# A two-block transformer kernel: x and ctx turned ahead of the first modulation, two projection chunks in the first stage

## The reference

```python
mod = (silu_c @ w_ada[l] + b_ada[l])[:, None, :]      # for x
mod_c = silu_cc @ w_ada[l] + b_ada[l]                 # for ctx
sh_a, sc_a, gt_a, sh_f, sc_f, gt_f = jnp.split(mod, 6, axis=-1)
csh_a, csc_a, ... = jnp.split(mod_c, 6, axis=-1)
h = rms_norm(x, g_attn[l]) * (1.0 + sc_a) + sh_a      # 256 tokens x 2048
hc = rms_norm(xc, g_attn[l]) * (1.0 + csc_a) + csh_a  # 256 tokens x 2048
pl, pc = h @ w_in, hc @ w_in                          # 2048 x 4928, split into q, k, v of four mixers
```

## Time and profile before

| | |
|---|---|
| three runs | 2822.24, 2824.46, 2827.69 us |
| span of the profiled execution | 2822.8 us |
| time of the profiled execution | not listed apart from its span |
| PE busy | 2748.1 us, 97% |
| VectorE busy | 1766.0 us, 63% |
| ScalarE busy | 1162.0 us, 41% |
| GpSimd busy | 388.5 us, 14% |
| moved by DMA | 579 MB, mean 205 GB/s |

### The profile page before, as it was taken

One profiled execution on the slowest core, in us unless ns is written; L12 is line 12 of the kernel. 1 busy time (PEld: TensorE's weight loads), 2 busy tenths in 40 slices (PEclk: granted clock), 3 DMA queues, 4 the chain that ended last, 5 costly groups with the idle time before them and its releaser, 6 DMA issues.

```text
span 2822.8 us, 33207 instructions
## 1 busy us (share of the span) xinstructions
PE 2748.1 (97%) x12531; PEld 2220.7 (79%) x12531; DVE 1766.0 (63%) x1952; ACT 1162.0 (41%) x1508; POOL 388.5 (14%) x297
## 2 busy tenths in 40 slices
PE   4999999999999999999999999999999999999998
PEld 1588887587887888888888888888888888888887
DVE  2379974766889655555574556544565656556566
ACT  3132224544444344444454544444444444444444
POOL 2214504101777200000040000000000000000000
PEclk9999999999999999999999999999999999999999
DMA  9988983246877555555555543655565656556663
GB/s 353 339 262 311 322 276 119 76 176 195 274 264 250 193 186 194 188 194 190 193 198 191 168 159 120 224 194 194 179 197 185 193 188 190 182 189 193 193 193 120
DMA packets 286236, 579.02 MB, mean 205 GB/s; under 512 B 14098, under 2 KB 18626, under 8 KB 283966
## 3 DMA queue, kind: packets, MB, share of 16 engines
q1 hardware_dynamic: 277240, 542.55, 58.1%
q0 software_dynamic: 7040, 34.29, 3.6%
q10 hardware_dynamic: 1862, 0.92, 0.1%
HBM read 572.59 MB, written 5.14 MB: 205 GB/s over the span
## 4 chain that ended last, share of the span: by engine, by line
PE 87%; DVE 5%; issue 4%; DMA 2%; POOLq 1%; POOL 1%; ACT 0%; DVEq 0%; SPq 0%; ACTq 0%
PE bank L367 27%; PE bank L369 26%; PE bank L368 26%; DVE w_lo L363 3%; DMA w_raw<-in_w_ada 1%; PE bank L628 1%; DMA b_rows<-in_b_ada 1%; PE bank L938 1%; PE bank L1943 1%; PE bank L460 1%; PE bank L790 0%; PE bank L654 0%; PE bank L827 0%; PE bank L1952 0%; PE bank L588 0%
## 5 line engine op out<-in xcount | busy, mean ns | idle before, releaser
L363 DVE TENSOR_TENSOR w_lo<-w_raw,w_hi 128x1024 fp32r<-128x1024 f32 (+2 forms) x856 | 1136.1, 1353 | 529.8 <-ACT w_hi L355 528.5
L355 ACT ACTIVATE w_hi<-w_raw 128x1024 fp32r<-128x1024 f32 (+2 forms) x856 | 889.0, 1054 | 1156.4 <-PE bank L369 1000.0
L367 PE MATMUL bank<-w_hi,xa_hi 128*128 128x512 f32 (+1 forms) x2304 | 905.9, 393 | 7.8 <-DVE w_lo L363 4.8
L369 PE MATMUL bank<-w_hi,xa_lo 128*128 128x512 f32 (+1 forms) x2304 | 895.6, 389 | 0.0
L368 PE MATMUL bank<-w_lo,xa_hi 128*128 128x512 f32 (+1 forms) x2304 | 895.1, 388 | 0.0
L367 PEld LDWEIGHTS bank<-w_hi,xa_hi 128*128 128x128 f32 x2304 | 433.2, 188 | 108.2 <-DVE w_lo L363 9.2
L369 PEld LDWEIGHTS bank<-w_hi,xa_lo 128*128 128x128 f32 x2304 | 433.1, 188 | 90.1
L368 PEld LDWEIGHTS bank<-w_lo,xa_hi 128*128 128x128 f32 x2304 | 433.3, 188 | 87.2 <-issue 0.7
L367 PE MATMUL bank<-w_hi,ffn_act_hi 128*128 128x512 f32 x800 | 311.5, 389 | 0.2 <-DVE w_lo L363 0.2
L368 PE MATMUL bank<-w_lo,ffn_act_hi 128*128 128x512 f32 x800 | 311.2, 389 | 0.0
L369 PE MATMUL bank<-w_hi,ffn_act_lo 128*128 128x512 f32 x800 | 311.2, 389 | 0.0
(11 more groups left out here) (306 smaller groups left out, 2037.7 us busy)
## 6 DMA issues: line engine op xcount, KB each, us to landing
w_raw<-in_w_in SPq DMA_DIRECT2D x116, 1024.0 KB, 5.1
w_raw<-in_w_ada SPq DMA_DIRECT2D x80, 1024.0 KB, 7.3
w_raw<-in_w_up SPq DMA_DIRECT2D x64, 1024.0 KB, 5.6
w_raw<-in_w_down SPq DMA_DIRECT2D x64, 1024.0 KB, 5.0
w_raw<-in_ffn_wg SPq DMA_DIRECT2D x44, 1024.0 KB, 5.2
w_raw<-in_ffn_wu SPq DMA_DIRECT2D x44, 1024.0 KB, 5.2
w_raw<-in_ffn_wd SPq DMA_DIRECT2D x44, 1024.0 KB, 5.1
w_raw<-in_w_out SPq DMA_DIRECT2D x32, 1024.0 KB, 5.1
```

The source lines that it names most:

```text
L355: act.activation(whi[:, slot, ks, 0:w], raw[:, q, ks, 0:w], ACT.Copy)\
L363: dve.tensor_tensor(wlo[:, slot, ks, 0:w], raw[:, q, ks, 0:w], whi[:, slot, ks, 0:w].bitcast(F32), ALU.subtract).then_inc(sem("lo_made"), 1)
L367: pe.matmul(out, xh, wh, start=first, stop=False)
L369: return pe.matmul(out, xl, wh, start=False, stop=last)
```

## The change

The two lists of the first stage change: each of four groups has two ada chunks, then the quarter of chunk 1 and that of chunk 0. Chunk 1 (512 columns, two token tiles, banks 6 and 7) leaves the mixed stage. x and ctx are scaled by VectorE, turned by PE without modulation into banks 0 to 3, 6 and 7, and copied to SBUF by ScalarE, all during the first two ada chunks. The scale and shift sums of a chunk are copied by ScalarE as rows; PE turns them into columns by four small products; VectorE adds b_ada and makes the scale (now one number per partition) and modulates turned x and ctx in place, 128 x 256 at a time. ScalarE then copies the high part and VectorE subtracts, from SBUF. The spread, GpSimd's products, the broadcast of g_attn and the b_ada rows are gone; g_attn and b_ada come in as 48 rows of 128 ahead of the identity and x on SP's queue, and are turned with c. The ada products alternate between banks 4 and 5.

```diff
-U_OUT = U_MIX + 4 * (len(WIN) - 1) + 4 * N_LATE_D + 4
+U_OUT = U_MIX + 4 * (len(WIN) - 2) + 4 * N_LATE_D + 4
...
-    for c in range(N_ADA_1):
-        if c >= 2 and c % 2 == 0:
-            loads.append(("win", 0, c // 2 - 1))
-        loads += [("ada", c, q) for q in range(4)]
-    return loads + [("win", 0, 3)]
+    for g in range(4):
+        loads += [("ada", c, q) for c in (2 * g, 2 * g + 1) for q in range(4)]
+        loads += [("win", 1, g), ("win", 0, g)]
+    return loads
...
-BY_VECTOR = {1: (1, 1, 1, 1), 2: (1, 1, 2, 1), 3: (1, 1, 1, 1), 4: (2, 2, 2, 2), 5: (2, 2, 2, 2), 6: (2, 3, 2, 3), 7: (3, 3, 3, 0)}
+PIECES = {g: [(1, 0), (1, 1), (0, 0), (1, 2), (1, 3), (0, 1), (0, 2), (0, 3)] for g in range(3)} | \
+    {3: [(1, 0), (1, 1), (0, 0), (0, 1), (0, 2), (0, 3), (1, 2), (1, 3)]}
+EARLY_BANK = {0: 0, 1: 6}
+EARLY_TOKS = {0: (0, 1, 2, 3), 1: (0, 1)}
+def early_count(w, g, j):
+    return 8 * g + PIECES[g].index((w, j)) + 1
+BY_VECTOR = {2: (2, 2, 2, 2), 3: (1, 1, 1, 1), 4: (2, 2, 2, 2), 5: (2, 2, 2, 3), 6: (2, 3, 2, 3), 7: (3, 3, 3, 0)}
```

On SP, when a slot is free again (`front_read`):

```diff
-                sp.wait_ge(sem("ada_used" if kind == "ada" else "early_lo"), 4 * c + q + 1 if kind == "ada" else 2 * q + 2)
+                if kind == "ada":
+                    sp.wait_ge(sem("ada_used"), 4 * c + q + 1)
+                else:
+                    sp.wait_ge(sem("early_lo"), 4 * q + (2 if c == 1 else 4))
...
+        def early_lo(dve, w, g, h):
+            q = FRONT.index(("win", w, g)) % 4
+            dve.wait_ge(sem("early_hi"), 4 * g + (1 if w == 1 else 3) + h)
+            dve.tensor_tensor(wlo[:, w, 2 * h:2 * h + 2, :], raw[:, q, 2 * h:2 * h + 2, :],
+                              whi[:, w, 2 * h:2 * h + 2, :].bitcast(F32), ALU.subtract).then_inc(sem("early_lo"), 1)
+        def early_piece(pe, w, g, j):
+            pe.wait_ge(sem("h_lo"), 2 * g + (1 if w == 1 else 2))
+            pe.wait_ge(sem("early_lo"), 4 * g + (1 if w == 1 else 3) + j // 2)
...
+        def modulate(dve, g, v):
+            for k in range(4 * g, 4 * g + 4):
+                m = dve.tensor_scalar(xt[v][:, k, :], xt[v][:, k, :], s_col[:, k, v:v + 1], b_col[:, k, v:v + 1],
+                                      ALU.mult, ALU.add)
+            m.then_inc(sem("h_made"), 1)
```

On ScalarE:

```diff
+            rows(0)
+            turn_x_act(act, 0)
+            turn_x_act(act, 1)
+            rows(1)
+            turn_x_act(act, 2)
+            turn_x_act(act, 3)
             for g in range(4):
-                early_hi(act, g)
-                turn_h_act(act, g)
+                if g:
+                    rows(2 * g)
+                    rows(2 * g + 1)
+                early_hi(act, 1, g)
+                h_hi(act, g, 0)
+                h_hi(act, g, 1)
+                early_hi(act, 0, g)
...
                 if i < 2:
-                    act.wait_ge(sem("early_used"), 4 * i + 12)
+                    act.wait_ge(sem("early_used"), early_count(i, 3, 3))
...
+                if i == 1:
+                    win_copy(1)
```

On VectorE:

```diff
+            for g in range(4):
+                take(2 * g)
+                take(2 * g + 1)
+                dve.wait_ge(sem("xt_copied"), 4 * g + 4)
+                modulate(dve, g, 0)
+                modulate(dve, g, 1)
+                early_lo(dve, 1, g, 0)
+                h_lo(dve, g, 0)
+                early_lo(dve, 1, g, 1)
+                h_lo(dve, g, 1)
+                early_lo(dve, 0, g, 0)
+                early_lo(dve, 0, g, 1)
```

On PE:

```diff
+            for q in range(4):
+                ada_unit(0, q)
+            columns(0)
+            for q in range(4):
+                ada_unit(1, q)
+                if q:
+                    turn_x_pe(pe, q - 1)
+            columns(1)
+            turn_x_pe(pe, 3)
+            pe.wait_ge(sem("xt_copied"), 16)
+            for g in range(3):
+                rest = list(PIECES[g])
+                for u in range(8):
+                    c, q = 2 * g + 2 + u // 4, u % 4
+                    ada_unit(c, q)
+                    if u < 5 or u == 7:
+                        w, j = rest.pop(0)
+                        early_piece(pe, w, g, j)
+                    if q == 3:
+                        columns(c)
+                for w, j in rest:
+                    early_piece(pe, w, g, j)
+            for w, j in PIECES[3]:
+                early_piece(pe, w, 3, j)
```

More of the change, by code:

```diff
@@ L95, in mixed_units @@
     units = []
-    for c in range(1, len(WIN)):
+    for c in range(2, len(WIN)):
         for q in range(4):
@@ L416, in early_piece @@
             m.then_inc(sem("early_used"), 1)
-        def turn_bank(g, i):
-            return 4 if g == 3 and i % 2 else 7
-        def turn_h_pe(pe, g, i):
-            pe.wait_ge(sem("h_ready"), 4 * g + i + 1)
-            wait(pe, "h_lo", 4 * g + i - (g == 3 and i >= 2))
-            for j in range(4):
-                m = pe.transpose(ps[turn_bank(g, i)][:, j * P:j * P + P],
-                                 xin[:, i, (4 * g + j) * P:(4 * g + j + 1) * P], ident[:, :])
-            m.then_inc(sem("h_turned"), 1)
@@ L448, in build, with h_lo @@
+        def h_lo(dve, g, v):
+            dve.wait_ge(sem("h_hi"), 2 * g + v + 1)
+            dve.tensor_tensor((XA, XB)[v][1][:, 4 * g:4 * g + 4, :], xt[v][:, 4 * g:4 * g + 4, :],
+                              (XA, XB)[v][0][:, 4 * g:4 * g + 4, :].bitcast(F32), ALU.subtract).then_inc(sem("h_lo"), 1)
         TURN = {"h2": range(8), "mrg": [0, 1, 2, 3, 2, 3, 4, 5], "h3": [2, 3, 6, 7, 6, 7, 4, 5], "h4": [4, 5, 6, 7] * 2}
@@ L1643, in _ @@
-            early_lo(dve, 3)
-            take(N_ADA_1 - 1)
-            for i in range(4):
-                turn_h_dve(dve, 3, i)
+                    .then_inc(sem("late_row"), 1)
+            dve.wait_ge(sem("x_rstd"), 1)
+            for g in range(4):
+                for i in range(4):
+                    x = xin[:, i, g * NCH:(g + 1) * NCH]
+                    dve.tensor_scalar(x, x, stat(RSTD + i), None, ALU.mult).then_inc(sem("x_scaled"), 1)
+            for g in range(4):
+                take(2 * g)
[9 more added lines that the diff above has]
+                early_lo(dve, 0, g, 1)
@@ L1944, in ada_unit, with columns @@
                                   start=q == 0, stop=q == 3)
                 m.then_inc(sem("ada_used"), 1)
-            def spread_row(c):
+            def columns(c):
                 pe.wait_ge(sem("ada_rows"), c + 1)
-                wait(pe, "mod_row", c)
-                for v in range(2):
-                    m = pe.matmul(ps[5 + v][:, :], pick[:, v:v + 1].to_broadcast([P, P]),
-                                  rows_1[:, c % 2, :], start=True, stop=True)
-                m.then_inc(sem("ada_combined"), 1)
@@ L1974, in _ @@
-            early_piece(pe, 2, 2)
-            spread_row(N_ADA_1 - 1)
-            early_piece(pe, 2, 3)
-            for i in range(4):
-                turn_h_pe(pe, 3, i)
-            for j in range(4):
-                early_piece(pe, 3, j)
+                for k in range(4):
+                    m = pe.matmul(ps[4 + c % 2][:, 2 * k:2 * k + 2], rows_1[:, c % 2, k * P:k * P + P], pick[:, :],
+                                  start=True, stop=True)
+                m.then_inc(sem("ada_columns"), 1)
@@ L2033, in _ @@
                     if cx is not None:
[L2034 removed]
+                        wait(pe, "late_row", sum(f < i for f in FOLD_AT))
                 toks = (0, 1) if cx is None else (0, 1, 2, 3)
```

217 lines of the change are left out of this document (83 added, 134 removed).

## The result

The changed kernel takes **2832.53 us** (median of 7 runs, 2830.22 to 2841.24); the kernel before, timed beside it, 2823.39 (2821.62 to 2827.69). The ratio is 1.0033, 95% interval 1.0022 to 1.0044: slower by more than 0.2%. I had forecast 2823.3, 1.2 us faster; it is 9.1 us slower. The profiled execution took 2831.79 us, its span is 2829.9, against a span of 2822.8: 7.1 us more.

The account below looks back on a forecast made before the run. PE, busy 97% of a 2822.8 us span, was taken as the bound. 4.3 us won by chunk 4 and 3.1 lost at chunk 5 gave -1.2 on 2824.46: 2823.3 us, own range 2817 to 2830, 8-in-10 range 2810 to 2833.

Parts of the forecast that it names:

- chunk 5's product: Thirteenth ada product returned to chunk 5, 3 instead of 2 behind its last quarter; no room on VectorE, 3.1 us lost.
- the period of the first stage: Time per group of first-stage loads, from ada(3,3) to ada(5,3) to ada(7,3): 29.6 us instead of 27.3.
- no difference behind: Expected trace sign: behind chunk 7's last quarter, 1 us earlier than before, the kernels show no difference.
- The start: Opening up to ada(3,3): first ada quarter lands near 23.2, last turn copied at 55.4, ada(3,3) used at 81.2.
- The slots: First-stage load buffers held until VectorE subtracts the win quarters: free at t + 9.2 and t + 12.6, so transfers run dry.
- t: End of the last ada product of a group, ada(2g+1, 3), in the first stage; later times count from it.
- the bracket on the double rate: Aside on modulating: by the skill, fp32 tensor_scalar runs at twice tensor_tensor's rate, so the lower sum, 1.9 us, holds.
- Rival B: First-stage chain longer still, PE at the lower clock: each period 3.6 us longer, start 4 us more, 2834.5 us; chance 0.17.
- rival A: First-stage transfers stay back to back: ada(7,3) at 124.5, chunk 4 at 209.9, 2807.4 us; chance 0.14.
- The end of the stage: PE's work behind the last ada product: 25.4 us, ending at 165.8 with chunk 1 finished, 14.2 us won.
- The mixed stage: Chunks 2 and 3: PE waits 7.1 us for chunk 0's copy, VectorE bounds, chunk 4 starts at 225.8, 4.3 us won.
- The sum: Whole kernel: 4.3 us won by chunk 4 and 3.1 lost at chunk 5, -1.2 us.

Follow-up runs that it names:

- own buffer: Changed kernel with the window loads of groups 1 and 2 in a separate 16 KB buffer per partition, not in the shared slots; ratio 0.9991 to the kernel before.
- less modulation: Changed kernel with only the first of each four modulating instructions left; ratio 1.0007 to the kernel before.
- copied first: Changed kernel with VectorE copying chunk 0 right behind its split of chunk 2's first quarter, ahead of the two ada products; ratio 1.0025 to the kernel before.
- the late kernel of before: Kernel before with 24 extra PE products ahead of chunk 0's last piece, delaying PE alone; ratio 1.0014 to the kernel before.
- four products ahead: Changed kernel with chunk 0's copy moved early and four ada products made before chunk 2; ratio 1.0001 to the kernel before.
- the kernel that differs from that one only further on: Kernel before with one ada product moved from chunk 2 to chunk 5; ratio 1.0008 to the kernel before.
- the first here: Kernel before with x and ctx turned ahead and modulated per partition, chunk 1 left in the mixed stage, second try; 2815.75 us against 2825.3.

## Why the prediction was wrong

The mechanism was right: the late slots lengthen the periods, chunk 2 waits for the copy, chunk 5's product costs some 3 us. What failed is the size of a term, the period of the first stage: 29.6 us forecast, 32.1 and 31.9 measured, 4.8 us in both. Luck hid 3.5 of them, since the start was better. Smaller errors of the same sign stand behind it, and "no difference behind" did not hold. The median is 10.3 us above the forecast; 5.5 of them are there at chunk 8 and are accounted for below, the rest arises behind it and stays in part open.

**The start** was better than I had it: ada(0,0) landed at 23.0 as forecast (23.2), but the last turn was copied some 4 us earlier (near 51 instead of 55.4), so ada(3,3) was used at 77.7 instead of 81.2. (The 69.3 that the prediction names beside it for the kernel before is the end of ada(3,2), 68.28 + 1.06; ada(3,3) started there at 72.84. Nothing is worked out from it.)

**The slots.** Mechanism right, size off. I gave a period 29.6 us; it has 32.1. The second slot comes free at t + 13.5, not t + 12.6: the eight modulating instructions take 2.6 us, where I had 1.9, and the columns on PE ahead of them 0.8 (80.52 to 81.33) for 0.5. The eight overlap by 0.08, as I had it, but one takes 0.41 and not 0.31: the duration between two one-scalar forms was the wrong guess. The trace of before has a one-scalar form on 128x256, at 0.35 (L868), which I overlooked. The lower sum that the bracket on the double rate names didn't come. From there to ada(5,3) it is 17.0 us, not 16.0. The last 0.6 us is the unit itself, 1.62 at the lower clock for 1.06. In the second period the clock delays the columns by another 1.0, and the second slot comes free at t + 14.6. So ada(7,3) is used at 141.8 for 140.4: the better start covered most of it. Rival B, the longer chain with a lower clock, was in part what happened. The waits for DMA are on the rows of ada(5,3); the experiments show the chain (own buffer: periods of 27.2 and 27.1; less modulation: some 2 us less in each). With its own buffer the transfers stay back to back, as rival A had it, but chunk 4 comes at 220.8 and not at 209.9: A took ada(7,3) at 124.5, counting from the first load, and the first group still waits for the turns.

**The end of the stage** is t + 26.3 instead of 25.4, F = 168.1 instead of 165.8: 2.3 us of the error.

**The mixed stage.** PE's pause ahead of chunk 2 is 7.32 us, forecast 7.1, with the releaser that I named; and it is covered, as I had it (copied first, chunk 4 stays). Chunk 4 at F + 61.6 instead of F + 60.0: 1.6 us more. VectorE starts on chunk 2 at F - 1.9 as forecast and reaches chunk 4's split 62.1 us later (166.23 to 228.37), not 60.7. I had put its waits at nothing; it has two, 0.57 for ScalarE and 0.46, and the other 0.4 are in the work itself.

**Chunk 5's product.** VectorE reaches the split in chunk 7 3.05 us later, forecast 3.1. But behind PE's two waits there (0.57 and 1.82) the clock is lower (0.76 from 385 to 392 us). That is 1.2 more by the profiles without the fall, and chunk 8's start loses 4.7 between chunks 4 and 8, not 3.1. I had counted the wait and not the clock behind it: 1.6 us in all, a few tenths of them open.

**The sum.** -1.2 + 2.3 + 1.6 + 1.6 = +4.3 at chunk 8, which is what the trace has. My own range held chunks 2 and 3 (up to +3) and each period (0 to +2.6), not the two periods together; the start, at -3.5, lay beyond its -2.

**Behind chunk 8** I forecast nothing, and the span shows 2.8, the medians some 4 to 5 us. 1.7 of the span is a lower clock at 511 us; the rest arises from 740 to 950 us. In nine profiles in which chunk 8 starts at 407.9 or earlier, the waits of that stretch come to 2.6 to 4.7 us, once to 7.3; in seven in which it starts later, to 4.9 to 10.9. That lateness does it fits these and the late kernel of before. It doesn't explain why kernels that start chunk 8 early also have medians 2 to 6 us above it, and what in that stretch doesn't move with PE, and so turns lateness into waits, was not tried. The cause stays open. The fall at 450 to 530 us came in nine of fourteen profiles of other kernels and in neither of the kernel before; the kernel before made late didn't have it. I can't say why.

## What to carry to other kernels

A load buffer that is released at the end of another engine's list ties the transfers to that whole list. Before windows and a modulation share four slots, ask when the last subtraction is done, and either give the windows a buffer of their own or put their split in time that the engine has idle: here a buffer of their own is worth 9 us at chunk 8 and takes the change from slower to no measurable difference from before. Work moved between stages should be priced at both places: in the kernel before, one product taken from where PE doesn't wait for VectorE saved nothing, and cost 4.2 us at its new place, the clock included. A gain at a later mark says nothing until the mark ahead of the edit is compared too. And where two parts come in one change, measure each alone: the first here is a gain of 9.6 us, once its window is split in time.

## What the runs showed of the hardware

A two-scalar tensor_scalar on 128x256 fp32 takes 0.41 us and follows the one before at 0.325 (four in 1.38, the next four 1.30 later). A one-scalar form of that size takes 0.35 in the trace of before (L868). Per column the two-scalar form is no faster than a subtraction: four take 1.30 for 1024 columns, one subtraction of 1024 columns 1.14 from start to start. The Trainium skill ("VectorE: DVE Perf Modes", the section on the TRN2 errata) has SBUF-source operations pay a fixed extra latency for each instruction. The 1.30 against 1.14 agrees with a fixed part for each, but one width alone doesn't part it from the rate.

PE's granted clock fell behind a pause in some executions and not in others with the same pause. Near ada(5,3), with waits of 1.5 to 1.7 us ahead, the unit took 1.62 in the first profile of the changed kernel and 1.06 with four products ahead. Among three waits of 1.1 to 1.5 us between 139 and 146 us it fell to 0.50 in both profiles of the kernel before. It stayed at 1.00 in the kernel that differs from that one only further on, which put chunk 2 some 2 us earlier. In chunk 7, behind 0.2 to 0.6 and 1.8 us, it fell in five of eight profiles, at 1.2 us each. The Trainium skill ("TensorE: Matmul & The Clock Gate", Part 1) has the chip look at activity in a window that runs free and doesn't reset with the kernel's start, and the traces agree that the same pause may or may not cost. In a chain of few instructions the price, where it came, was 1.0 us (columns 3.8 us behind the ada unit instead of 2.8).
